# RWKV head loop: the projection steps of a turn stand at other places between the small products, and layer 1 projects key, receptance, value

## The reference, cut to what matters

```
r, k, v, wl, al, gl = split(p + mu * bi_shift(p))        # p = (normed input) @ w_in
w = -softplus(-(w0 + tanh(wl) @ w2)) - 0.5 ;  decay = exp(-exp(w))
a = sigmoid(a0 + al @ a2) ;  g = sigmoid(gl) @ g2
kk = heads(k * k_k) / norm ;  k_dir = k * (1 + (a - 1) * k_a)
step: S = S * w_t - (S kk_t) (kk_t a_t)^T + v_t k_t^T ;   y_t = S r_t
out = ((groupnorm(y) + bonus(r, k, v)) * g)
```

## Time and profile before

| | us |
|---|---|
| median of 3 runs (lowest, highest) | 3791.62 (3789.88, 3792.77) |
| the profiled execution | 3793.02 |
| its span in the trace | 3791.2 |
| TensorE busy (share of span) | 3443.3 (91%) |
| VectorE, ScalarE, GpSimd busy | 1638.9, 1047.5, 673.9 |
| mean granted TensorE clock | 0.972 of full |

### The profile page before, as it was taken

How to read it: one execution, slowest core, us unless ns; L and a number is a source line. 1 busy time by engine, 2 the same in 40 slices (tenths; PEclk the granted TensorE clock), 3 DMA queues, 4 the chain that set the end, 5 groups by cost and what they waited for, 6 DMA issues and landing times. The chain is left out here.

```text
span 3791.2 us, 93086 instructions
## 1 busy us (share of the span) xinstructions
PE 3443.3 (91%) x41918; PEld 1967.0 (52%) x41918; DVE 1638.9 (43%) x2944; ACT 1047.5 (28%) x1842; POOL 673.9 (18%) x583
## 2 busy tenths in 40 slices
PE   6999999998999978999999698998999998799997
PEld 3454445545666665443332345656666666684333
DVE  3584704655666652121000356814166666522111
ACT  2211003304455451111111321104155555311001
POOL 0141201303333331010000012103023334200000
PEclk8999999999999999999999799999999999899998
DMA  5104523431101010349998211833311110058996
GB/s 199 67 1 135 187 67 86 160 101 27 35 22 28 19 48 24 124 176 420 409 390 346 88 55 55 260 108 79 91 33 30 28 36 28 26 217 360 424 424 273
DMA packets 238879, 538.71 MB, mean 142 GB/s; under 512 B 49264, under 2 KB 157056, under 8 KB 205584
## 3 DMA queue, kind: packets, MB, share of 16 engines
q1 hardware_dynamic: 219424, 463.98, 33.4%
q0 software_dynamic: 19056, 68.69, 5.2%
HBM read 514.75 MB, written 17.87 MB: 140 GB/s over the span
## 5 line engine op out<-in xcount | busy, mean ns | idle before, releaser
L1303 PE MATMUL banks<-sb_h,sb_ring 128*128 128x512 f32 (+1 forms) x1344 | 474.8, 512 | 11.3 <-DMA sb_ring<-w_branch 7.6
L1797 PEld LDWEIGHTS banks<-inv 64*64 64x64 f32 x15104 | 309.1, 139 | 181.0 <-issue 178.5
L1797 PE MATMUL banks<-inv 64*64 64x64 f32 x15104 | 342.3, 226 | 62.2 <-issue 27.8
L1303 PEld LDWEIGHTS banks<-sb_h,sb_ring 128*128 128x128 f32 x1344 | 254.3, 190 | 225.0 <-issue 196.1
L1806 PE MATMUL banks<-sb_h,sb_ring 128*128 128x512 f32 (+1 forms) x672 | 330.2, 599 | 8.1 <-DMA sb_ring<-w_in 4.1
L823 PE MATMUL banks<-sb_h,sb_ring 128*128 128x512 f32 x512 | 233.3, 614 | 19.4 <-SPq L245 19.4
L823 PEld LDWEIGHTS banks<-sb_h,sb_ring 128*128 128x128 f32 x512 | 100.2, 198 | 139.8 <-issue 119.0
L2497 DVE COPY inv<-banks 128x512 f32<-128x512 f32 x144 | 98.5, 691 | 169.3 <-PE banks L1797 168.5
L3150 PE MATMUL banks<-gu,xs 128*64 128x512 f32 x768 | 168.9, 594 | 2.7 <-DMA gu<-gu_pairs 2.2
L1303 PE MATMUL banks<-sb_branch,sb_ring 128*128 128x512 f32 (+1 forms) x512 | 170.9, 487 | 0.0
L3302 DVE TENSOR_TENSOR hrow<-hrow,banks 128x256 f32<-128x256 f32 x36 | 15.1, 421 | 356.2 <-ACT hrow L3338 356.2
(11 more groups left out here) (478 smaller groups left out, 5676.8 us busy)
## 6 DMA issues: line engine op xcount, KB each, us to landing
gu<-gu_pairs SPq DMA_DIRECT2D x64, 1536.0 KB, 16.5
gu<-gu_tiles SPq DMA_DIRECT2D x57, 1024.0 KB, 9.3
sb_ring<-w_in SPq DMA_DIRECT2D x24, 2048.0 KB, 9.3
sb_ring<-gu_tiles SPq DMA_DIRECT2D x39, 1024.0 KB, 9.4
vtok<-w_mod POOLq DMA_DIRECT2D x64, 512.0 KB, 5.5
sb_ring<-down_pairs SPq DMA_DIRECT2D x32, 1024.0 KB, 14.7
sb_ring<-w_in SPq DMA_DIRECT2D x26, 1024.0 KB, 5.4
sb_ring<-down_tiles SPq DMA_DIRECT2D x25, 1024.0 KB, 8.6
```

The lines of the kernel that those rows point to most:

```text
L1303: mm = nc.tensor.matmul(out, left(kt), right(kt), start=kt == 0, stop=kt == KT - 1)
L1797: m = mm(k.bank[bank][H[to], at:at + w], left, right, start=start, stop=True, skip_group_check=True)
```

## The change

In both layers, steps are dealt anew over the same turn: 24 steps, as before. The step behind `inverse(b, 3)` moves into `gate_and_norm`, between the gate's matmul and the norm's. One more step each stands behind `gram_times_v` and behind `inverse(b, 7)`. In `crossing`, the two steps behind `step(b, 1)` are gone and `step(b, 2)` comes after `value_turns`; one step of two goes ahead of `step(b, 5)` and ahead of `gram_pair(c, 0, 0)`; and one step each is new behind `gram_other` and behind `gram_turned`. In layer 1 (`t0` not 0) the passes are key, receptance, value instead of key, value, receptance, with receptance in bank 5 and value in bank 7.

```
-STEP_ORDER = (1, 2, 0)
-        FIRST_BANK, RAW_BANK = (5, 7, 1), (7, 7, 5)
+        FIRST_BANK = (5, 7, 1)
+        STEP_ORDER, RAW_BANK = ((1, 0, 2), (5, 7, 7)) if t0 else ((1, 2, 0), (7, 7, 5))
...
-            def gate_and_norm(c, b=None):
+            def gate_and_norm(c, b=None, filler=None):
                 pe.wait_ge(s.wa_in, c(4, 4))
                 mm(k.bank[GATE_BANK][:, 0:n], g2[:], low[:, 1, t0:], start=True, stop=True).then_inc(s.gate, 1)
                 pe.wait_ge(s.gate, c(1, 1))
                 pe.sem_inc(s.low_free, 1)
+                if b:
+                    filler(1)
                 pe.wait_ge(s.kksq, c(1, 1))
...
                     step(b, 1)
-                    filler(2)
-                    step(b, 2)
                 if c:
                     hold(s.rawin, kept)
                     value_turns(c)
                 if b:
+                    step(b, 2)
                     filler(1)
                     step(b, 3)
...
                     key_turns(c, 1)
                 if b:
-                    filler(2)
+                    filler(1)
                     step(b, 5)
...
                 if b:
-                    filler(2)
+                    filler(1)
                 if c:
                     hold(s.rdec, c(2, 2))
                     gram_pair(c, 0, 0, [(s.tok, c(8, 5)), (s.tok, c(8, 6))])
...
                     gram_other(c)
                     if b:
+                        filler(1)
                         hold(s.sq, b(1, 1))
                     gram_turned(c)
+                    if b:
+                        filler(1)
                     for part in range(2):
                         gram_pair(c, 1, part, [] if part else [(s.gevac, c(6, 2)), (s.gevac, c(6, 2))], s.gdone)
...
                 inverse(b, 3)
-                filler(1)
                 if c:
-                    gate_and_norm(c, b)
+                    gate_and_norm(c, b, filler)
...
                 gram_times_v(b)
-                filler(1)
+                filler(2)
...
                 inverse(b, 7)
-                filler(1)
+                filler(2)
                 apply_inverse(b)
...
                 if project:
-                    keep(2, c, b(3, 8))
+                    keep(STEP_ORDER[1], c, b(3, 8))
...
                 if project:
-                    keep(0, c, b(3, 9))
+                    keep(STEP_ORDER[2], c, b(3, 9))
```

## The result

The changed kernel takes 3800.85 us (median of 20 runs, 3792.57 to 3807.59) against 3791.72 (20 runs, 3788.11 to 3798.44): 1.0023 times as long, 95% interval 1.0016 to 1.0029, or 9 us (6 to 11). One execution of this study, one of e3's, fell in a slow state (5890.98 us at a granted clock of 0.553); the ratios leave it out. The page, and four stretches in the columns of the earlier trace rows: two turns of layer 0, one of layer 1, and the Gram end that had a clock of 1.00 before.

What follows compares the result with a forecast made beforehand. TensorE was taken as the bound, through its idle time and slow stretches, with "issue" stops read as instruction loading. Layer 0's -3.2 plus layer 1's +9.6 gave +6.4 on 3793.0, 3799.4, less 1.4 for the median: 3798.0 us, range 3778 to 3811.

Steps and rivals of the forecast that it cites:

- The wait at the second pair: Ahead of the second Gram pair: TensorE waits for copies queued behind ScalarE's late keep, 1.7 to 1.8 us layer 0, 1.3 layer 1.
- The chain: Layer 0, `chunk_products` to first Gram pair: fewer steps save 3.64 us per turn, -3.0 after 0.6 is given back.
- the give-back for density: Layer 0, `chunk_products` to first Gram pair: denser stretch meets instruction loading and returns 0.6 us per turn (0 to 1.8).
- The stretch ahead of it: Layer 0, gate to `chunk_products`: two steps more +1.72, `apply_inverse`'s wait -0.66, loading -0.2; together +0.9 us per turn, +0.6 in stopped turns.
- the gain at the stopped turns: Layer 0's two turns with a 2.33 us stop in `gram_turned`: stop and low clock go, -2.2 us each.
- the low clock's 1.3 us: Layer 0's stopped turns, Gram pair behind `gram_turned`: 3.39 us falls to 2.08 once the clock no longer drops.
- ScalarE's part: Layer 1, first to second Gram pair: 0.8 us of the +2.9 per turn is a longer wait for ScalarE.
- the stretch behind the pair: Layer 1: stop in the pair goes, -0.7; stage 0 stop stays about 1.6, -0.2; together -0.9 us per turn.
- the middle and the chain, twice "-0.2": Layer 1, `gram_times_v` to `chunk_products` and the chain behind: narrow and wide steps trade places, each -0.2 us per turn.
- the last rival: Loading is hidden: "issue" stops are fixed and stay, only waits count; +2.2 us per layer 1 turn, 3804 us, chance 0.1.
- Loading gains more: Rival: steps spare the instruction loading stops everywhere, -5 us in layer 1, -7 in layer 0; 3780 us, chance 0.25.
- The clock in all turns: Rival: waits ahead of the second pair drop TensorE's clock in all twelve turns, +12 us; 3810 us, chance 0.2.

Runs made afterwards that it cites:

- e3: Kernel before, with only one late step each in `crossing` moved behind `gram_other` and `gram_turned`; 3803.49 us, ratio 1.0021.
- e4: Changed kernel, with ScalarE's keep of the third pass behind `receptance_grams` instead of ahead of it; 3786.18 us, ratio 0.9987.
- e5: Kernel before, with ScalarE's keep of the third pass behind `receptance_grams`, dealing unchanged; 3791.88 us, ratio 0.9997.
- e11: Changed kernel, with layer 1 dealt and ordered as before and ScalarE's keep where it was; 3785.32 us, ratio 0.9987.
- e1: Changed kernel, with layer 1's old pass order (key, value, receptance), new dealing kept; 3802.02 us, ratio 1.0023.
- e6: Kernel before, with 128 already fulfilled semaphore waits (64 instructions more) on TensorE ahead of layer 1's turns; 3805.62 us, ratio 1.0036.
- e8: e4, with SP's third weight load of a turn put off until the next inverse's first product, small loads ahead of it; 3775.16 us, ratio 0.9951.
- e10: Kernel before, with only the third 512 KB load of a turn held back until the next turn's first product; 3783.86 us, ratio 0.9981.
- e12: The study's fastest kernel (3767.85 us), with one wide step of layer 1 moved from between inverse stages 6 and 7 to ahead of stage 0; 3784.89 us, ratio 0.9975.
- e2: Kernel before, with only layer 1's pass order changed to key, receptance, value; 3802.42 us, ratio 1.0027.

## Why the prediction was right, and where it was not

I predicted 3798.0 us, slower the likeliest; 3800.85 was measured, inside the range. The wait at the second pair was foreseen with its cause; that both layer sums came out near owes something to luck. By place, in us over each layer:

| | layer 0 predicted | measured | layer 1 predicted | measured |
|---|---|---|---|---|
| first step behind stage 0 to `chunk_products` | +4.8 | +0.3 | -1.2 | -6.5 |
| `chunk_products` to the first pair | -18.2 | -18.2 | -1.2 | +7.4 |
| first pair to the second | +12.8 | +14.8 | +17.4 | +17.9 |
| second pair to the first step behind stage 0 | -2.6 | +0.2 | -5.4 | -6.6 |
| ahead of the first of these and behind the last | 0 | -0.7 | 0 | -0.8 |
| sum | -3.2 | -3.6 | +9.6 | +11.4 |

*The second pair.* Predicted: a wait of 1.7 to 1.8 us in layer 0 and 1.3 in layer 1, +2.4 and +2.9 us from pair to pair. Measured: 1.76 and 1.33, 8.09 for 5.51 and 7.31 for 4.40 where nothing else stops. The reason (a keep at the head of an engine that works in order) is shown by e4, which takes the keep away from there and the wait with it, and by e5, where there is no late step and nothing to gain.

*Layer 0.* Predicted -3.2 us, measured -3.6 in the profile and -5 by e11. The sum is right by luck in part. The chain was right, with the give-back for density as stops in `chunk_products`. The stretch ahead of it came out 4.5 us better, above all because the norm's wait for the gate (1.9) was not in my sum and `gram_times_v` to `chunk_products` lost 2.5 us of "issue". The second pair was 2.0 worse. And the gain at the stopped turns failed: the stop in `gram_turned` went and the Gram pair behind it takes 2.25 us for 3.39, but stage 0 now stops for 1.01 us, and from the second pair to the first step behind stage 0 it is 6.22 us for 6.31. I had put the low clock's 1.3 us there as a gain. These two turns take 75.31 and 74.55 us where they took 75.16 and 75.50; I had -2.2 for each, and all turns at about 72 to 73 us. The two kinds are still there, from 71.50 to 75.31.

*Layer 1.* Predicted +9.6, measured +11.4 in the profile and +14 by the runs. ScalarE's part is right (+0.8 per turn; measured 5.0 us in all), and so is the stretch behind the pair (-0.9; measured -1.1 per turn from the second pair to the first step behind stage 0), though its stop was 1.0 to 1.5 us and not 1.5 to 1.8. The step that failed is the one on the middle and the chain, twice "-0.2". The middle came out at -0.6, but the chain at +1.2: I held that VectorE's waits, which the narrow steps uncover, fall into time that loading takes anyway. They cost 7.3 us more in all, nearly what the last rival had put on them one by one (0.25 + 0.5 + 0.44 per turn, 7.1 in six). And what loading gave up behind the pair it took again in the chain: "issue" fell by 3.6 us behind the pair, rose by 4.3 in the chain, and as a whole fell by 0.6 us. That made 1.0 us per turn too little. Against it stand 2.9 us of the layer that I had not counted, from the first step behind stage 0 to `gram_times_v`: the wait for the gate (1.8) is gone, and so are two stretches at half clock (1.5 each), of which the turn of the earlier trace rows at 0.97 had one; the rest of that stretch grew by 1.9. So here too the sum owes something to errors that cancel.

*Why VectorE's waits don't hide in loading.* e1 and the changed kernel have the same length in layer 1, one with 31.8 of "issue" and 1.5 of VectorE, the other with 20.8 and 10.0. The two do stand in for each other. The error was to take the kernel before as a case where the stretch was already as long as loading wants it: it had 21.4 and 2.7 already, and the dealing of before hid more of both. That last half is argued from these sums and not tested by itself.

*The rivals.* Loading gains more (3780): no, in layer 1 "issue" fell by only 0.6 us. The clock in all turns (3810): no, three turns at 0.98 where there were six, and 1.00 over the turns that wait 1.33 and then stop for 1.43 us in layer 1, and over five of the six that wait 1.76 us in layer 0. In the sixth it did fall behind that wait (969.63 above), so the rival's mechanism exists and was rare. What decides between the six these rows don't show. Loading hidden (3804): its price for the waits of layer 1 was the better one, its reason is refuted: e6 moves the stops with the stream, and e8 and e10 shorten them by 1.1 and 1.4 us with a load that no TensorE instruction there waits for. The Trainium skill, "Runtime: NRT & Kernel Launch", section "Instruction fetch mechanics", says that fetching is hidden. These traces don't agree: the stops are 21 us of layer 1 before. The chances in the prediction add up to 0.35 for the same and 0.41 for slower, not 0.33 and 0.43.

*Still open.* 2 us of e12's chain, half of e3's loss, and the 6 us of e6 outside layer 1. And one profile of each kernel can't tell how often the clock falls in it, so e8's and e10's gain is not split between shorter stops and a clock that falls less often.

## What to carry to other kernels

Before work is put in front of a wait, ask what the engine that is waited for does next in its own order: two steps put ahead of a wait only pushed it out here, because a copy of their result stood in front of what the pair needed, and a swap of two calls on ScalarE gave 14 us back. Narrow and wide filler are not alike: the wide ones belong where another engine's latency has to be covered, and exchanging them cost 10 us with no step moved (e2). Where a dense stretch of small products shows "issue" stops at the same place of the instruction stream turn after turn, look first at which large load runs beside it; moving that load gained 7 to 14 us by the ratios, with no product moved. Where a sum of many small parts comes out right, compare it part by part before trusting it: in layer 0 two misses of 4.5 and 4.8 us cancelled.

## What the runs showed of the hardware

- TensorE's stops by "issue" in dense 64x64 stretches lie at fixed places of the stream: put 64 instructions in, and they move by 64 in three turns; in the two others, where the clock is at half, stage 0 has no stop (e6).
- A 512 KB load beside such a place lengthens the stop: 2.77 us for 1.67 (e4 and e8), and 2.33 for 0.96 (before and e10). In e4 the instruction packet starts only as the load ends, 6.2 us after the one before it, in e8 4.8.
- Where 64 instructions stand that only wait for a fulfilled semaphore, TensorE is idle for 6.64 us, 0.10 us for each (e6).
- The granted clock stayed at 1.00, the 2.4 GHz level, in five of the six Gram ends of layer 0 with 1.76 us of waiting, and was 0.51 from 970.00 to 973.40 in the sixth; before, a Gram end with a stop of 2.33 us had 0.76.
